# Attention pass of a hybrid decoder step: keys and queries transposed by head, scores read out from two wide tiles

## The reference, cut to what matters

```python
s = einsum('bqhmd,bshmd->bhmqs', q, k) * 64 ** -0.5
s = where(k_pos <= q_pos, s, -inf)
p = softmax(s, axis=-1)
w = p[:, :, 0] - lam * p[:, :, 1]
o = einsum('bhqs,bshd->bqhd', w, v)
```

## Time and profile before

| | us |
|---|---|
| median of 3 runs | 1947.1 |
| lowest, highest | 1947.05, 1949.76 |
| span of the profiled execution | 1952.1 |
| attention in it: first transposes to last output rows | 1098 to 1545 |

### The profile page before, as it was taken

How to read it: one execution, slowest core, us unless ns; L and a number is a source line. 1 busy time by engine, 2 the same in 40 slices (tenths; PEclk the granted TensorE clock), 3 DMA queues, 4 the chain that set the end, 5 groups by cost and what they waited for, 6 DMA issues and landing times. The chain is left out here.

```text
span 1952.1 us, 26730 instructions
## 1 busy us (share of the span) xinstructions
PE 1690.2 (87%) x9364; PEld 1396.3 (72%) x9364; DVE 1112.7 (57%) x2447; ACT 776.8 (40%) x1133; POOL 601.3 (31%) x684
## 2 busy tenths in 40 slices
PE   3899999993699999999999579999889558859998
PEld 2788888882588888888888467778777545547776
DVE  7322222216587786877877489999878451143332
ACT  4333333323445445454454345666555313131111
POOL 8211112226535546456364212111020030012221
PEclk9899999996799999999999789999999878979999
DMA  6211111115100000000000410110000284334442
GB/s 201 78 66 64 64 64 64 64 43 173 54 17 28 22 27 16 21 27 21 27 16 12 172 49 34 33 34 34 17 6 7 76 276 130 120 115 151 150 142 74
DMA packets 70142, 136.13 MB, mean 70 GB/s; under 512 B 8114, under 2 KB 14770, under 8 KB 70066
## 3 DMA queue, kind: packets, MB, share of 16 engines
q1 hardware_dynamic: 70066, 135.13, 20.7%
HBM read 96.31 MB, written 38.80 MB: 69 GB/s over the span
## 5 line engine op out<-in xcount | busy, mean ns | idle before, releaser
L116 PE MATMUL h_proj<-h_w_hi,h_xT_hi 128*128 128x512 f32 x544 | 225.8, 415 | 16.6 <-DVE h_xT_lo L663 14.6
L116 PE MATMUL a_proj<-a_w_hi,a_xT_hi 128*128 128x512 f32 x544 | 218.6, 402 | 12.1 <-DVE a_xT_lo L308 10.5
L116 PE MATMUL h_proj<-h_w_hi,h_xT_lo 128*128 128x512 f32 x544 | 217.1, 399 | 0.0
L116 PE MATMUL h_proj<-h_w_lo,h_xT_hi 128*128 128x512 f32 x544 | 217.0, 399 | 0.0
L116 PE MATMUL a_proj<-a_w_lo,a_xT_hi 128*128 128x512 f32 x544 | 216.7, 398 | 0.0
L116 PE MATMUL a_proj<-a_w_hi,a_xT_lo 128*128 128x512 f32 x544 | 216.4, 398 | 0.0
L429 POOL TENSOR_TENSOR h_stage_or_levels<-h_stage_or_levels,h_qT 128x128 f32<-128x128 f32 x192 | 106.1, 553 | 266.9 <-ACT h_stage_or_levels L600 266.9
L1143 PE MATMUL p_ops<-p_V,p_WT 128*128 128x128 f32 x1088 | 148.1, 281 | 11.9 <-ACT p_WT L1006 11.3
L996 ACT ACTIVATE p_scores<-p_scores,p_nmx 128x128 f32<-128x128 f32 (+15 forms) x128 | 153.2, 1197 | 10.3 <-DVE p_nmx L1052 9.2
L1006 ACT ACTIVATE p_WT<-p_tps 128x512 f32<-128x512 f32 (+3 forms) x160 | 84.7, 531 | 170.7 <-PE p_tps L1130 170.6
L1143 PEld LDWEIGHTS p_ops<-p_V,p_WT 128*128 128x128 f32 x1088 | 133.4, 193 | 19.6 <-ACT p_WT L1006 19.3
(11 more groups left out here) (241 smaller groups left out, 3683.3 us busy)
## 6 DMA issues: line engine op xcount, KB each, us to landing
a_xt<-in_x SPq DMA_DIRECT2D x17, 512.0 KB, 3.6
h_xt<-in_x SPq DMA_DIRECT2D x17, 512.0 KB, 3.4
a_stage<-in_w_in SPq DMA_DIRECT2D x16, 512.0 KB, 3.7
h_stage_or_levels<-in_w_in SPq DMA_DIRECT2D x16, 512.0 KB, 3.8
s_kc<-in_cache_k SPq DMA_DIRECT2D x32, 256.0 KB, 3.6
s_vc<-in_cache_v SPq DMA_DIRECT2D x32, 256.0 KB
y_xt<-in_x SPq DMA_DIRECT2D x16, 512.0 KB, 4.5
out_y_p<-y_yt SPq DMA_DIRECT2D x16, 512.0 KB, 3.0
```

What stands on the lines that cost most here:

```text
L116: mm = eng.matmul(out, a[:, k, :], b[:, k, cols], start=(k == 0 and a is x_hi and b is w_hi), stop=(k == KD - 1 and a is x_lo))
```

## The change

Keys and queries are transposed as they are loaded: a head's 128 columns hold both maps, so 8 transposes a tile do, into one `sps` tile. The split moves to the read-out: ScalarE copies the high part from PSUM (K into its own half of the partitions, then Q), VectorE subtracts for the low part (K into the other half, Q in place), four instructions of 64 partitions on each. The query's other half is filled by two transfers from SBUF to SBUF (`both_halves`, on SP). POOL keeps nothing in this pass but one memset. `sps` becomes two tiles of 1024 columns, and a read-out takes up to 1024 columns of one map. TensorE's inner loop now goes over column group and map. The mask and zero tiles grow to 1024 columns, and the coefficient is made by another instruction form.

```diff
-        sps = [ps(f"sps{n}", [P, 512]) for n in range(4)]
+        sps = [ps(f"sps{n}", [P, WIDE]) for n in range(2)]
@@ sync @@
+            def both_halves(i):
+                sp.wait_ge(s["sps_read"], first_prep[i] + 1)
+                for m in range(2):
+                    sp.dma_start(f32(QS[i % 2][other[m], m])..., f32(QS[i % 2][own[m], m])...)
+            both_halves(0)
             for i in range(NP + 1):
+                if i + 1 < NP:
+                    both_halves(i + 1)
@@ gpsimd @@
-                pool.tensor_tensor(k_hl[:, :, 1], ..., ALU.subtract)
-                pool.tensor_tensor(q_hl[:, 1], ..., ALU.subtract)
@@ scalar, split_hi(i): now in the step of head 2, ahead of its exp_row @@
-                act.activation(k_hl[:, :, 0], qk_in[...], ACT.Copy)
-                act.activation(q_hl[:, 0], twice(qk_in[...]), ACT.Copy)
+                act.wait_ge(s["sps_full"], k + 1)
+                for m in range(2):
+                    mm = act.activation(KT[own[m], m, :, cols], src, ACT.Copy)
+                mm.then_inc(s["k_hi"], 1)
+                for m in range(2):
+                    mm = act.activation(QS[i % 2][own[m], m, 0], src, ACT.Copy)
+                mm.then_inc(s["q_hi"], 1)
@@ vector, prep_out(i) @@
-                for n in range(6):
-                    dve.tensor_copy(dst, src).then_inc(s["sps_read"], 1)
+                dve.wait_ge(s["k_hi"], i + 1)
+                for m in range(2):
+                    dve.tensor_tensor(KT[other[m], m, :, cols], src, f32(KT[own[m], m, :, cols]), ALU.subtract)
+                dve.wait_ge(s["q_hi"], i + 1)
+                for m in range(2):
+                    mm = dve.tensor_tensor(QS[i % 2][own[m], m, 1], src, f32(QS[i % 2][own[m], m, 0]), ALU.subtract)
+                mm.then_inc(s["sps_read"], 1)
@@ vector, rows(n) @@
-                for c, (c0, w) in enumerate(chunks[i]):
+                for c, (c0, w) in enumerate(spans[i]):
@@ tensor, prep(i) @@
-                pe.wait_ge(s["k_lo"], i + 1)
-                pe.wait_ge(s["q_lo"], i + 1)
-                for n in range(6):
...
+                for n in range(2):
+                    for h in range(H):
+                        mm = pe.transpose(sps[k % 2][...], qk_in[:, i % 2, 1 - n, h * P:(h + 1) * P], ident[:, :])
@@ tensor, scores and the loop over a head @@
+                    pe.wait_ge(s["q_twice"][i % 2], 32 * (i // 2 + 1))
+                pe.wait_ge(s["sps_read"], k - 1)
-                n_s = len(chunks[tile_head[n][0]]) if n < n_heads else 0
+                n_s = 2 * len(spans[tile_head[n][0]]) if n < n_heads else 0
-                for c in range(max(n_s, n_v)):
+                for c in range(max(n_s, n_v + 1)):
                     if c < n_s:
-                        scores(n, c)
+                        scores(n, c // 2, c % 2)
```

More of the change, by code:

```diff
@@ L924, in pass_attention @@
         block = open_block(nc, ctx, s.values())
+        spans = [[(c, min(WIDE, (i + 1) * P - c)) for c in range(0, (i + 1) * P, WIDE)] for i in range(NP)]
         chunks = [[(c, min(512, (i + 1) * P - c)) for c in range(0, (i + 1) * P, 512)] for i in range(NP)]
@@ L933, in pass_attention @@
                 first_prep[i + 1] = n_use
-                n_use += 6
+                n_use += 1
             first_sc[i, h], first_wt[i, h] = n_use, n_wt
-            n_use += 2 * len(chunks[i])
+            n_use += 2 * len(spans[i])
             n_wt += len(chunks[i])
-        def twice(q):
-            return q.rearrange("p (m d) -> p m d", d=DQ)[:, :, None, :].broadcast_to([P, M, 2, DQ])
+        own = [slice(0, DQ), slice(DQ, P)]
+        other = own[::-1]
         @block.sync
@@ L969, in _ @@
             pool.memset(zero[:, :], 0.0).then_inc(s["zero"], 1)
[L970 to L978, removed]
         @block.scalar
@@ L1108, in scores @@
-            def scores(n, c):
-                i, h = tile_head[n]
-                c0, w = chunks[i][c]
-                if c == 0:
-                    pe.wait_ge(s["sps_read"], first_prep[i] + 6)
-                for m in range(2):
-                    k = first_sc[i, h] + 2 * c + m
-                    pe.wait_ge(s["sps_read"], k - 3)
+                pe.wait_ge(s["qk_load"][i % 2], 32 * (i // 2 + 1))
+                k = first_prep[i]
+                if k >= 2:
+                    pe.wait_ge(s["sps_read"], k - 1)
@@ new lines, in prep, with scores @@
+                for n in range(2):
+                    for h in range(H):
+                        mm = pe.transpose(sps[k % 2][:, (4 * n + h) * P:(4 * n + h + 1) * P], qk_in[:, i % 2, 1 - n, h * P:(h + 1) * P], ident[:, :])
+                mm.then_inc(s["sps_full"], 1)
+            def scores(n, c, m):
+                i, h = tile_head[n]
+                c0, w = spans[i][c]
+                if c == 0 and m == 0:
+                    pe.wait_ge(s["sps_read"], first_prep[i] + 1)
+                    pe.wait_ge(s["q_twice"][i % 2], 32 * (i // 2 + 1))
+                k = first_sc[i, h] + 2 * c + m
+                pe.wait_ge(s["sps_read"], k - 1)
+                for b0 in range(0, w, 512):
+                    b1 = min(b0 + 512, w)
@@ L1160, in _ @@
                         values(n - 2, c - 1)
-                if n_v and max(n_s, n_v) == n_v:
-                    values(n - 2, n_v - 1)
 def pass_samples(nc, io, keep):
```

84 lines of the change are left out of this document (36 added, 48 removed).

## The result

| | before | after |
|---|---|---|
| time, median (range), us | 1948.3 (1947.1 to 1949.8) | 1971.5 (1969.8 to 1974.4) |
| ratio, 95% interval | | 1.0121 [1.0100, 1.0141] |
| span of the profiled execution | 1952.1 | 1967.9 |
| attention: first load to the last weights on VectorE | 447.0 | 473.8 |

The changed kernel takes 23.2 us more, where 13 were forecast: inside the bounds given, 1941 to 1975, but above the forecast's own range of 1952 to 1969. In the two profiles attention is 26.7 us longer. What follows it runs the same code but was shorter, 407.0 us against 414.5, at a mean granted clock of 0.92 for 0.90.

A forecast was written before the change was run, and what follows sets the result against it. In attention neither TensorE nor VectorE is free, so their order within each head was taken to decide. Gains and losses summed to +13 on the median 1947.1, forecasting 1960 us, own range 1952 to 1969, outer bounds 1941 to 1975.

The forecast's parts named there:

- Large tiles, +17: Tiles 8 to 11: second map's last scores wait behind more transposes and values, 1.05 us a head, 17 us more.
- Tiles 12 to 15, +8: The last, wide read-out starts only after its last matmul, 0.5 us a head over 16 heads, 8 us more.
- Tiles 0 to 7, +4: First group's transposes stand between the two maps: 3 us more in tiles 4 to 7, 1 in tiles 0 to 3.
- Preparation on DVE, -8: Four subtractions (2.45 us) replace six copies (3.6 us): 8 us less over seven preparations of tiles 8 to 14.
- Start, +4: First scores wait for Q's copies, queued behind the values: 5.5 us later, 1.5 given back by the second preparation.
- POOL's wait -4, POOL beside DVE -13, old falls -5: Gone with POOL's work: PE's wait for its split, 4 us; lengthened DVE instructions, 13; clock falls in tiles 12-14, 5.
- New falls, +9: TensorE idles 2.05 us at preparations; its clock falls at six in ten of preparations 5 to 15, 9 us more.
- the clock holds: Rival: TensorE's idle times at preparations bring no fall, clock stays at 2.4 GHz; 1950 us, chance 0.15.
- POOL cost more: Rival: POOL's work cost 20 us instead of 13, clock holds, head loops lose 4 less; 1939 us, chance 0.12.
- Reads were the bound everywhere: Rival: VectorE's own work falls by 40 us and all of it counts; 1907 us, chance 0.03.
- The clock falls at every preparation: Rival: falls at every preparation, clock staying low in tiles 0 to 3, cost 23 us, not 9; 1974 us, chance 0.15.

The follow-up runs named there:

- run 3: Changed kernel plus 16 unused transposes in each head after a preparation, tiles 4 to 14, to keep TensorE busy: 1961.7 us, ratio 1.0058.
- run 5: New preparation alone, with the read-outs, four PSUM tiles and score order of the kernel before: 1936.9 us, ratio 0.9941 to the kernel before.
- run 9: New preparation with the old read-outs, plus only the first quarter of the values queued ahead of the first Q's copies: 1927.1 us, ratio 0.9896.
- run 2: Changed kernel with all four loads of the values queued behind the copies of the first Q: 1969.9 us, ratio 1.0108.
- run 10: Changed kernel with only the first quarter of the values queued ahead of the copies of the first Q: 1972.0 us, ratio 1.0121.
- run 7: Changed kernel with both maps' scores together only in tiles 8 to 15, not in heads behind a preparation: 1955.8 us, ratio 1.0037.
- run 11: Changed kernel with two POOL subtractions on a scratch tile, started with the weights of the last heads of tiles 0 to 14: 1975.7 us, ratio 1.0143.
- run 4: Changed kernel with two POOL subtractions on a scratch tile, started from the exponentials of each tile's first head: 1975.7 us, ratio 1.0135.

## Why the prediction was right and wrong

The direction and the main mechanism were right; two terms of the sum were mis-sized, and a small one was left out. Term by term, in attention:

- **Large tiles, +17: right.** With the clock held (run 3), tiles 8 to 11 take 131.8 us, with narrow read-outs (run 5) 114.6: 17.2.
- **Tiles 12 to 15, +8: right.** 158.9 against 152.8 is 6.0, and run 5 has a fall behind tile 14's preparation that run 9 has not (13.09, 11.49), 1.6: 7.6.
- **Tiles 0 to 7, +4: right.** Tiles 4 to 7 84.9 against 82.3, the small ones (after against run 5, without tile 0) 1.2: 3.8.
- **Preparation on DVE, -8: the step that failed.** It was to shrink from 3.6 us to 2.5 in seven tiles, and to cost nothing more in four. It went from 3.51 to 2.85 there (-4.6 in all), and from 3.50 to 3.92 in preparations 5 to 8 (+1.7): -2.9. The subtractions run strictly one behind the other, 2.79 for four where I took 2.45, and the six copies had overlapped the weights by 0.09, which I left out: 0.43 in each of eleven preparations, 4.7 of the 5.1 that are missing. My bound of -6 for subtractions without overlap counted seven of the eleven.
- **Start, +4: the other step that failed.** It cost 9.7. I set the first scores at 1110, and they came at 1109.4, but the pass had begun 3.5 us earlier than in the profile before: counted from its first load it is 22.2 against 14.0, not 5.5 but 8.2 later. The copies took 11.6 to land, as forecast (11.0 and 0.7); what I had wrong is when they are issued. I put them in the place of a load that was issued 7.7 after the pass's first load (1098.36), but they wait for the first subtractions and went out 10.0 after it (1097.15). And the second preparation gave nothing back: PE waits 3.6 us for its subtractions, and tile 0 took 1.5 more where I had 1.5 less. Up to the end of tile 3, run 2 takes 6 us of it away and run 10 7, by the order of the queue alone.
- **POOL's wait -4, POOL beside DVE -13, old falls -5: right in sum.** No run takes POOL's work away alone; run 5 against before is the nearest. In it the heads behind the preparations of tiles 1 to 3 are 3.9 us shorter, and the heads of tiles 1 to 14 without a preparation (first and last ones) 17.6: 21.5 for 22.
- **New falls, +9: nearly right.** 11.4 by run 3: eight falls at the eleven preparations where I took 6.6, at 1.4 each on average, as forecast. PE's idle time at a preparation is 2.17 us in tiles 8 to 14, 2.05 by the forecast, and 2.8 to 3.0 in tiles 4 to 7. That six in ten came near is partly luck: nothing in the forecast says at which preparations the clock falls, and the falls of run 10 are at others.

17.2 + 7.6 + 3.8 - 2.9 + 9.7 - 21.5 + 11.4 = 25.3, of the 26.7 that the profiles show. The two failed terms are 10.8 of the 13.7 by which the sum fell short. Most of the last 1.4 is in heads that no term covers: the third heads of tiles 1 to 14 and the four of tile 15 are 1.9 us longer in run 5 than before, 0.05 in most of them. That is what the coefficient's new form adds, 0.273 us long where the old one usually took 0.219; the forecast put its cost at nothing.

Of the rivals, *the clock holds* and *POOL cost more* fell with runs 3 and 5. *Reads were the bound everywhere* fell with the busy table: DVE does 31 us less and the pass is longer. The Trainium skill's rule (VectorE: DVE Perf Modes, "The TRN2 errata"), a fixed cost per instruction, has its 0.08 us in the trace, but it does not say what waits: here DVE waits for scores. *The clock falls at every preparation* came nearest in time, for another reason: its falls cost 11.4, not 23, and there were none in tiles 11, 13 and 14. Its second condition came true in tiles 0 and 1, at a price that no run shows apart: over the first 53.5 us of the pass the mean clock was 0.50, where before it was 0.71.

What was to be seen was seen in the large tiles (waits of 0.34 and 0.88 for 0.4 and 0.9, a head of 7.02 for 7.0), and in tile 5 a wait of 0.44 for 0.5 to 0.7. The long instances are gone (L1067 is the successor of L1059, L1070 that of L1063; ns min, median and max):

```profile
L1067 DVE TENSOR_SCALAR p_coef<-p_rl,p_ls,nlam x64: 272/273/276, 1112.3 to 1558.3; 128x1 f32<-128x1 f32 x64
```

The weights of 1536 columns take 1818 ns on average where they took 2334. Only the preparation was longer than forecast: 2.85 for 2.5, and 3.92 for 3.6 in tiles 4 to 7.

## What to carry to other kernels

Fewer and wider read-outs gain nothing where the reader waits for the producer. Ask what then stands in the producer's order between the reads: here a group of transposes and values between two maps cost 1.1 us a head in tiles 8 to 11 (run 3 against run 5), and putting both maps together there took it back in heads without a preparation (run 7). Behind a preparation the loss stayed. That two large PSUM tiles let TensorE run ahead less than four small ones is the likely reason, but no run changed the number of tiles alone. Try the two halves of such a change apart: here one gained 0.6%, and the other lost 2.6% alone. Count a first transfer from the pass's own start, and try it ahead of bulk loads that nobody needs yet: that took 7 us out of attention twice (runs 9 and 10), though in run 10 the rest of the program took 6 us longer.

## What was not expected of the hardware

POOL and DVE, where DVE's instruction has two inputs in SBUF as the weights have, took turns and did not share: a POOL subtraction behind long weights took 3.01 us for 1.14 (run 11), weights behind POOL 3.88 for 1.82 (before). Read-outs from PSUM kept their length beside POOL (758 and 757 ns, run 4). The Trainium skill states it so (SBUF — State Buffer, "SBUF: two separate sides"): whichever starts first keeps the shared port for its whole instruction, and a DVE instruction with two inputs in SBUF is among those affected. The traces agree.

Four subtractions on half the partitions take 0.689 us each and never overlap (22.0 us for 32, both lines), where the copies of before had a pair in 1.28. The Trainium skill's rule on operands in other quadrants (VectorE: DVE Perf Modes, "Two Vector instructions with no wait between them") agrees; no run here had them on equal halves.

A fall of the clock needed little, and the length of the idle time alone does not tell where one comes. In the changed kernel an idle of 2.17 us brought a fall in tiles 8 to 10 and 12 and none in tiles 11, 13 and 14; run 10 has falls in tiles 10 to 13 instead, behind the same 2.17. Two idles of 0.92 and 0.69 around a short stretch of work passed (run 5, tile 9), and 0.76 and 0.68 brought a fall (run 5, tile 14). Tile 11 of the changed kernel, timeline and busy table:

```profile
1374.03 1.20 PE L1120 MATMUL p_sps<-p_KT,p_Q 128*128 128x512 f32 x4 [2.17 <-DVE p_Q L1039]
```
```profile
1371.00:1376.00 5.00, 2.63 (x17) 2.16 (x18) 4.87 (x8) 4.94 (x8) 0.00 (x0) 1.00 0.19 39
1376.00:1381.00 5.00, 4.63 (x34) 3.90 (x32) 3.24 (x10) 2.16 (x3) 0.00 (x0) 1.00 0.61 174
```
